# Seven products for eight in half of an input projection

## The reference

```python
xn = _rmsnorm(x, n1g)
z = xn @ w_in                       # 2048 x 6152: convolution B, C, x; q, k, v, o; two gates
bg, cg, xt, q, k, v, o, ig, fg = jnp.split(z, _SPLIT_IDX, axis=-1)
conv = causal_conv3(cg * xt);  y_conv = _rmsnorm(bg * conv, conv_g)
h, C1, n1, m1 = _mlstm_chunked(q, k, v, ig + b_i, log_sigmoid(fg + b_f), C0, n0, m0)
y_ml = sigmoid(o) * _rmsnorm(h, ml_g)            # per head, 4 heads
x = x + concat([y_conv, y_ml]) @ w_out
hn = _rmsnorm(x, n2g)
x = x + (silu(hn @ wg) * (hn @ wu)) @ wd         # feed-forward, 5632 wide
```

## Time and profile before

| | |
|---|---|
| median of 3 runs | 2466.73 us (2466.65 to 2467.93) |
| profiled execution, its own time | 2466.16 us |
| its span, first to last instruction | 2464.4 us |
| TensorE busy, matmuls | 2444.1 us (99%), 17544 |
| VectorE busy | 1760.1 us (71%) |
| ScalarE busy | 894.7 us (36%) |
| memory traffic | 132 GB/s over the span |

### The profile page before, as it was taken

The page is one execution under the profiler, slowest core; times in us unless marked ns, Lnnn a source line. Parts: engine busy times, 40 slices in busy tenths (PEclk is TensorE's granted clock), DMA queues, the critical chain, the costliest instruction groups (busy, mean ns, idle before and its releaser), DMA issues.

```text
span 2464.4 us, 44130 instructions
## 1 busy us (share of the span) xinstructions
PE 2444.1 (99%) x17544; PEld 2380.3 (97%) x17544; DVE 1760.1 (71%) x2453; ACT 894.7 (36%) x1235; POOL 48.3 (2%) x79
## 2 busy tenths in 40 slices
PE   9999999999999999999999999999999999999998
PEld 8999999999999998999999999999999999999886
DVE  7576585675687678778877877787777866866535
ACT  5222222122233335443344344434344533544313
POOL 0010000000000000000000000000000000000100
PEclk9999999999999999999999999999999999999999
DMA  5443343343336575443443434434334655745822
GB/s 132 118 132 89 114 120 95 85 134 95 105 101 184 174 210 174 120 120 111 128 119 104 128 111 121 118 112 121 117 101 116 246 153 160 264 129 144 286 73 77
DMA packets 459979, 329.09 MB, mean 134 GB/s; under 512 B 14407, under 2 KB 429283, under 8 KB 457425
## 3 DMA queue, kind: packets, MB, share of 16 engines
q1 hardware_dynamic: 403704, 250.29, 34.7%
q10 hardware_dynamic: 51448, 58.42, 7.6%
q0 software_dynamic: 4640, 17.73, 2.1%
HBM read 268.02 MB, written 58.37 MB: 132 GB/s over the span
## 4 chain that ended last, share of the span: by engine, by line
PE 60%; DVE 1%; ACT 0%; issue 0%; DVEq 0%; ACTq 0%
PE ps L838 17%; PE ps L842 17%; PE ps L840 17%; PE ps L853 2%; PE ps L956 2%; PE ps L958 2%; PE ps L960 2%; PE ps L983 0%; PE ps L964 0%; PE ps L965 0%; DVE oplo L2153 0%; PE ps L865 0%; DVE gw_ring L2140 0%; DVE dwlo L2409 0%; ACT ophi L1314 0%
## 5 line engine op out<-in xcount | busy, mean ns | idle before, releaser
L838 PE MATMUL ps<-ophi,gw_ring 128*128 128x288 f32 x3208 | 950.4, 296 | 5.0 <-DVE up L2197 3.5
L840 PE MATMUL ps<-oplo,gw_ring 128*128 128x288 f32 x3208 | 947.0, 295 | 0.0
L842 PE MATMUL ps<-ophi,gw_ring 128*128 128x288 f32 x3208 | 945.4, 295 | 0.0
L838 PEld LDWEIGHTS ps<-ophi,gw_ring 128*128 128x128 f32 x3208 | 602.4, 188 | 6.1 <-DVE up L2197 3.9
L842 PEld LDWEIGHTS ps<-ophi,gw_ring 128*128 128x128 f32 x3208 | 604.9, 189 | 0.0
L840 PEld LDWEIGHTS ps<-oplo,gw_ring 128*128 128x128 f32 x3208 | 603.1, 188 | 0.1
L1039 ACT ACTIVATE whi<-wraw 128x512 fp32r<-128x512 f32 x256 | 160.6, 632 | 576.2 <-PE ps L608 369.1
L605 PE MATMUL ps<-xhi,whi 128*128 128x288 f32 x1536 | 332.3, 298 | 0.5 <-DVE wlo L1612 0.5
L608 PE MATMUL ps<-xhi,wlo 128*128 128x288 f32 x1536 | 328.6, 296 | 0.0
L605 PE MATMUL ps<-xlo,whi 128*128 128x288 f32 x1536 | 328.5, 295 | 0.0
L2140 DVE TENSOR_TENSOR gw_ring<-graw_a,gw_ring 128x1024 fp32r<-128x1024 f32 x191 | 233.6, 1223 | 111.4 <-ACT gw_ring L1292 110.8
(11 more groups left out here) (339 smaller groups left out, 2669.9 us busy)
## 6 DMA issues: line engine op xcount, KB each, us to landing
wraw<-in_w_in_dram SPq DMA_DIRECT2D x96, 512.0 KB, 3.9
graw_a<-in_w_ffn_gate_dram SPq DMA_DIRECT2D x59, 512.0 KB, 3.7
graw_a<-in_w_ffn_up_dram SPq DMA_DIRECT2D x59, 512.0 KB, 4.7
graw_a<-in_w_ffn_down_dram SPq DMA_DIRECT2D x42, 512.0 KB, 5.8
wraw<-in_w_out_dram SPq DMA_DIRECT2D x32, 512.0 KB, 4.0
opraw<-hop SPq DMA_DIRECT2D x14, 1152.0 KB, 11.5
graw_b<-in_w_ffn_gate_dram SPq DMA_DIRECT2D x29, 512.0 KB, 3.8
graw_b<-in_w_ffn_up_dram SPq DMA_DIRECT2D x29, 512.0 KB, 4.7
```

The source lines that it names most:

```text
L838: pe.matmul(out, gw_ring[:, slot, 0, k, :], ophi[p][:, k, :], start=start and k == 0, stop=False, skip_group_check=True)
L840: pe.matmul(out, gw_ring[:, slot, 0, k, :], oplo[p][:, k, :], start=False, stop=False, skip_group_check=True)
L842: mm = pe.matmul(out, gw_ring[:, slot, 1, k, :], ophi[p][:, k, :], start=False, stop=k == GK - 1, skip_group_check=True)
```

## The change

The column tiles of a head are taken in six pairs: (q, k), (v0, v1), (o0, o1), (C, x) of group 0, (B of group 0, C of group 1), (x, B) of group 1. In 18 of the 24 pairs (`seven`) half of the K tiles, those of quarters 0 and 1, are multiplied as 2 x 2 blocks: rows are the two column tiles, the inner index is the quarter (0 or 1), columns are the two halves of the tokens. Seven products of blocks, each four K tiles by 288 columns, replace eight. Quarters 2 and 3 (d0, d1 of the first tile, d2, d3 of the second) are multiplied as before. The slots of a pair and the weight block of each:

The other six pairs keep eight quarters of 24 matmuls. A p slot has 12 matmuls, a d slot 24. TensorE's part:

```diff
+            def half_product(n, name, bank, start, stop, ready=None):
+                pe.wait_ge(lo_done, n + 1)
+                if ready:
+                    pe.wait_ge(*ready)
+                ...
+                for k in range(4):
+                    pe.matmul(out, whi[:, w, k, :], hi[:, k, :], ...)
+                    pe.matmul(out, whi[:, w, k, :], lo[:, k, :], ...)
+                    mm = pe.matmul(out, wlo[:, w, k, :], hi[:, k, :], ...)
+                mm.then_inc(w_used, 1)
+
+            def seven_pair(h, p, early=None, mid=None):
+                ...
+                before = (tile_read, i + 1) if not seven(*PLAN[PLAN.index((h, p)) - 1]) else (a_read, 2 * g)
+                pe.wait_ge(tile_read, i)
+                half_product(n, "p1", "c", True, False)
+                half_product(n + 1, "p0", "a", True, False, before)
+                direct_part(n + 2, 2, (("b", 0, True, False, None), ("c", 1, False, False, (copy_q, 3 * g + 1))))
+                if early:
+                    early()
+                half_product(n + 3, "p2", "a", False, False, (copy_q, 3 * g + 2))
+                half_product(n + 4, "p3", "b", False, False)
+                direct_part(n + 5, 3, (("b", 0, False, True, None), ("c", 1, False, False, None)))
+                if mid:
+                    mid()
+                half_product(n + 6, "p4", "a", False, False, (copy_q, 3 * g + 3))
+                half_product(n + 7, "p5", "c", False, True)
+                direct_part(n + 8, 2, (("d", 1, True, False, (tile_read, i + 1)), ("a", 0, False, False, (a_read, 2 * g + 1))))
+                half_product(n + 9, "p6", "a", False, False)
+                direct_part(n + 10, 3, (("a", 0, False, True, None), ("d", 1, False, True, None)))
```

The banks are a = 0, d = 1, b = 2, c = 3. ScalarE copies bank c after p1 and bank a after p0 and p2 (`copy_bank`, counted by `copy_q`), multiplies the norm gain into six of the eight weight quarters (`quad_gain`, four instructions of 128x128 each) and makes eleven high parts. VectorE makes the sums of weight blocks (`weight_total`), the gains of d0 and d1, eleven low parts, and builds the four result blocks:

```diff
+            def quad_gain(h, p, name):
+                ...
+                for k in range(4):
+                    ins = act.mul(raw_slot[j][:, k, :], raw_slot[j][:, k, :], vecs[:, col + k:col + k + 1])
+                ins.then_inc(quad_ok, 1)
...
+                def c11(h, p, out):
+                    slot_done(slot_of(h, p, "d1"))
+                    dve.wait_ge(copy_q, 3 * g + 2)
+                    link(tt(p1s[:], ps[:, 2, 0:HT], p1s[:], ALU.add))
+                    return out(p1s[:], 0)
+                def u3(h, p):
+                    slot_done(slot_of(h, p, "p4"))
+                    tt(p5s[:], ps[:, 0, 0:HT], p5s[:], ALU.add).then_inc(a_read, 1)
+                def c12(h, p, out):
+                    slot_done(slot_of(h, p, "p5"))
+                    link(tt(u2s[:], ps[:, 3, 0:HT], u2s[:], ALU.add))
+                    evac(out(u2s[:], 1))
+                def c21_c22(h, p, out):
+                    slot_done(slot_of(h, p, "d3"))
+                    out(ps[:, 0, 0:HT], 0).then_inc(a_read, 1)
+                    dve.wait_ge(a_read, 2 * g + 1)
+                    link(tt(p5s[:], ps[:, 1, 0:HT], p5s[:], ALU.add))
+                    evac(out(p5s[:], 1))
```

The order is written out by `step(h, p, s)`, which on VectorE does what slot s + 5 of the pair needs (a sum or a gain) and then the low part of slot s + 4; on ScalarE the bank copy, the high part of slot s + 4, and after some a `quad_gain` for a later slot. Pairs 3, 4 and 5 on VectorE, in a head with `seven(h, 3)` (steps without side work are joined):

```diff
+                    step(h, 3, 0)            # then conv_columns(0), states(), step 1, normaliser_parts(),
+                    ...                      # step 2, values_by_sample(), step 3
+                    steps(h, 3, 4, 5)
+                    first_half(h, 3, by_root(cg))
+                    steps(h, 3, 6, 7)
+                    c12(h, 3, by_root(cg))
+                    gate_again(6)
+                    step(h, 3, 8)
+                    denominator()
+                    step(h, 3, 9)
+                    c21_c22(h, 3, by_tile(cg, cg))
+                    step(h, 3, 10)
+                    outputs_of_head()
+                    step(h, 4, 0)
+                    conv_prompt(0, T)
+                    step(h, 4, 1)
+                    conv_sample(0)
+                    step(h, 4, 2)
+                    conv_scaled(0)
+                    step(h, 4, 3)
+                    sample_update()
+                    steps(h, 4, 4, 5)
+                    ...
+                    steps(h, 5, 2, 3, 4, 5)
+                    link(c11(h, 5, by_tile(cg, cg)))
+                    conv_prompt(0, HT)
+                    u3(h, 5)
+                    step(h, 5, 6)
+                    mixed_heads()
+                    step(h, 5, 7)
+                    c12(h, 5, by_tile(cg, cg))
+                    conv_prompt(HT, T)
+                    step(h, 5, 8)
+                    conv_sample(1)
+                    conv_scaled(1)
+                    step(h, 5, 9)
+                    c21_c22(h, 5, by_tile(own_conv(1), cv))
+                    step(h, 5, 10)
```

More of the change, by code:

```diff
@@ new lines, in hybrid_trunk_step @@
+    N_GAIN = len(GAINS)
+    QUADS = ("a21", "a22", "a11", "a12", "d2", "d3")
+    SUMS = ("p1", "p2", "p4", "p5")
+    NQ = 6
+    LOADS, free_at, loads_of = [], [0] * NQ, [0] * NQ
+    RAW_AT = {}
+    for h, p in PLAN:
+        if seven(h, p):
+            order = (("a21", "p4"), ("a22", "p6"), ("a11", "p4"), ("d0", "d0"), ("a12", "p5"), ("d1", "d1"),
+                     ("d2", "d2"), ("d3", "d3"))
+        else:
+            order = tuple((s, s) for s in QUARTERS)
+        for name, until in order:
+            j = min(range(NQ), key=lambda j: free_at[j])
+            loads_of[j] += 1
+            LOADS.append((h, p, name, j, free_at[j]))
+            RAW_AT[h, p, name] = j, 16 * loads_of[j]
+            free_at[j] = slot_of(h, p, until) + 1
@@ new lines, in gemm @@
+                for n in range(KT):
+                    w = ring(n0 + n // 4)
+                    if n % 4 == 0:
+                        pe.wait_ge(lo_done, n0 + n // 4 + 1)
+                    if n in between:
+                        between[n]()
+                    if ready:
+                        ready(n)
+                    k, (out, first, last) = ks[n], where[n]
+                    for moving in (hi, lo):
+                        for a in halves:
+                            pe.matmul(out[:, a, :], whi[:, w, n % 4, :], moving[:, 2 * k + a, :],
+                                      start=first and moving is hi, stop=False)
+                    for a in halves:
+                        mm = pe.matmul(out[:, a, :], wlo[:, w, n % 4, :], hi[:, 2 * k + a, :],
+                                       start=False, stop=last)
+                    if n % 4 == 3:
+                        mm.then_inc(w_used, 1)
@@ new lines, in direct_part @@
+            def direct_part(n, q, parts):
+                pe.wait_ge(lo_done, n + 1)
+                w = ring(n)
+                for bank, a, start, stop, ready in parts:
+                    if ready:
+                        pe.wait_ge(*ready)
+                    out = ps[:, BANK_T[bank], 0:HT]
+                    for s in range(4):
+                        k = 2 * (4 * q + s) + a
+                        pe.matmul(out, whi[:, w, s, :], xhi[:, k, :], start=start and s == 0, stop=False,
+                                  skip_group_check=True)
+                        pe.matmul(out, whi[:, w, s, :], xlo[:, k, :], start=False, stop=False, skip_group_check=True)
+                        mm = pe.matmul(out, wlo[:, w, s, :], xhi[:, k, :], start=False, stop=stop and s == 3,
+                                       skip_group_check=True)
+                mm.then_inc(w_used, 1)
@@ new lines, in steps, with hi_out @@
+            def steps(h, p, *which):
+                for s in which:
+                    step(h, p, s)
+            def hi_out(n, q):
+                if q < 2:
+                    act.wait_ge(raw_in[q // 2], n * 16 + 16)
+                else:
+                    act.wait_ge(gained, n * 2 + (N_GAIN + q - 1))
+                act.wait_ge(w_used, n * 4 + (N_IN + q + 1))
+                act.activation(whi[:, q], wraw[:, q // 2, 4 * (q % 2):4 * (q % 2) + 4, :], ACT.Copy).then_inc(hi_done, 1)
@@ L1213, in _ @@
+                mix_high(14)
+                squares_of_y(1)
+                mix_high(15)
+            for h in range(H):
+                round_of_head(h)
             act.wait_ge(rows_out, 1)
```

1234 lines of the change are left out of this document (767 added, 467 removed).

## The result

The changed kernel takes 2472.49 us (median of 18 runs, 2468.07 to 2475.02), the kernel before 2467.01 us in the same sessions (18 runs, 2466.06 to 2468.9): the ratio is 1.0021, 95% interval 1.0014 to 1.0028. It is slower by 5.5 us, just past the 0.2% named ahead. The forecast was 2463 us, range 2441 to 2476, with more chance on faster than on slower: the time lies in the range, on the side that had 0.24.

The account below looks back on a forecast made before the run. TensorE, busy 99% and issuing without holes, was taken as the bound: 2466.16 - 28.8 (matmuls) + 21.6 (waits) + 2.6 (clock) + 1 (late loads) = 2462.6; the runs' median stands 0.6 above that execution, so 2463 us, range 2441 to 2476.

Parts of the forecast that it names:

- the 0.2% named ahead: Threshold for no change: 4.9 us; faster meant below 2461.8 us, slower above 2471.7 us.
- the side that had 0.24: Chance given to slower than 2471.7 us: 0.2 from Rival (c) and 0.04 from rival (b); faster had 0.46.
- 28.8 us less for 216 matmuls: TensorE in 18 of 24 pairs: 12 matmuls fewer per changed pair, each saving 0.1333 us.
- An ordinary pair holds: Changed pairs without long side work: VectorE keeps up, with 1.9 us of slack before the next pair's sum.
- Rival (c): ScalarE becomes the bound in every changed pair, at the a22 quarter before the next pair's sum: 2478 us, chance 0.2.
- TensorE waits 4.5 us, in three heads: 13.5 us: End of pair 5: next pair's p0 waits for VectorE's C21 read, at 17.3 us where 12.8 is allowed.
- 1.4 + 0.2 + 0.8 + 0.3 = 2.7, three heads: 8.1 us: Pair 3 into 4: TensorE waits 1.4 at p0, 0.2 for `h_ok`, 0.8 at d2; u3 0.3 late.
- Late loads, "I take 1": Behind state store and spill, an 8 us landing pushes pair 4 by some 1.7 us; bounds 0 and 5, taken 1.
- The clock, "I take the middle, 2.6": Half clock after the three pair-5 waits, 1.7 us lost in one earlier event; bounds 0 and 5.1, taken 2.6 us.
- rival (b): All long waits drop the clock and loads come late: 2465 to 2468 us, no change, chance 0.23.
- signs named ahead: 17328 matmuls; pair-5 waits of 4.5 us then clock 0.5; 1.4 and 0.8 in pair 4; VectorE over 75%, ScalarE near 60%.
- three signs that were to show the forecast wrong: Pair-5 waits under 2 us; waits named after ScalarE's high parts or weight DMAs; spacing inside a product not 0.1333 us.

Follow-up runs that it names:

- one move out of pair 5: Changed kernel with the head's final products (`mixed_heads`) moved from pair 5 into the first step of the next head's pair 0: 2458.71 us, ratio 0.9966.
- work in the wait: Changed kernel with TensorE transposing a constant tile 30 times between p1 and p0 of pair 0, heads 1 to 3: 2467.32 us, ratio 1.0000.
- reordering only: Changed kernel with three VectorE moves: u3 of pair 5 earlier, state updates in two groups, first reciprocal behind pair 3's last evacuation: 2469.23 us, ratio 1.0007.
- state store later: Changed kernel with the sample-state store one pair later and a head's second spill behind the mixed outputs' signal: 2472.39 us, ratio 1.0017.
- C21 first: Changed kernel with pair 5's C21 scaled and read out of bank 0 before the second half's taps and sample taps: 2466.17 us, ratio 0.9995.
- buffer free early: C21 first, plus the sum for C22 written early into another buffer so `p5s` is freed: 2455.42 us, ratio 0.9955.
- and the transfers moved: Buffer free early, plus rows spread and spill behind pair 4's last low part and state store after step 7 of pair 5: 2447.32 us, ratio 0.9912.
- all that proved free: Kernel of "and the transfers moved" plus the three moves of "reordering only"; `mixed_heads` stays in pair 5: 2443.82 us, ratio 0.9903.
- everything in VectorE's list: Changed kernel with `mixed_heads` in next pair 0, C21 first, the "reordering only" moves, and sample-state products after p3; stores stay: 2460.76 us, ratio 0.9973.
- and the transfers: Everything in VectorE's list, plus rows spread and spill after pair 4's last low part, state store after step 7 of pair 5: 2452.51 us, ratio 0.9938.
- and the buffer free: Kernel of "and the transfers" plus early C22 sum in another buffer, head's outputs after p3's low part, sample-state products after d1: 2457.46 us, ratio 0.9963.
- more work for ScalarE: Changed kernel with each scaled copy on ScalarE done in two halves of 64 columns: 2481.22 us, ratio 1.0058.

## Why the forecast was wrong, by its own steps

- **28.8 us less for 216 matmuls** held. An undisturbed changed pair shows it: pair 1 of heads 1 to 3 takes 26.22 us instead of 27.96, pair 2 26.64 instead of 28.36, both 1.7 less, where twelve matmuls make 1.6.
- **"An ordinary pair holds"**, by 1.9 us, held: no wait in pairs 1 to 3, and 4.4 us more of ScalarE work lengthened them by 0.5 us at most. Rival (c) is out.
- **"TensorE waits 4.5 us, in three heads: 13.5 us"** held in size (12.65) and place. The reason was right as far as it went: work ahead of the read of C21. The forecast took all of it as having to stand there. It did not: with two releases (bank 0 and `p5s`) earlier in the same list the waits went, and no work had to leave. That `p5s` held a second wait behind the first was not seen.
- **"1.4 + 0.2 + 0.8 + 0.3 = 2.7, three heads: 8.1 us"** became 8.6: 1.24 at p0, 1.62 at d2, nothing at the other two.
- **Late loads, "I take 1"** is the step that failed most. I put the landing of 8 us behind the store and the spill on pair 4; it fell on pair 5, on d0, a quarter that VectorE must scale itself before the low part of p0 and the read of bank 0 can follow in its list. It cost 1.2, 0.6 and 1.7 us at p0 and then another 1.0 at u3, 6.4 us by the trace and 8.1 by the run with the transfers moved, for the 1 us of the sum. The upper bound was 5.
- **The clock, "I take the middle, 2.6"**: all three long waits were followed by half clock, 5.1 us by the records, 5.2 by the run that filled the waits. One event had shown the full price, and the middle stood on no row.
- Left over: 1.7 us outside the heads' stage, 0.6 ahead of it and 1.1 in the feed-forward stage. That stage, which no kernel here changes, takes 1537.5 to 1540.3 us in the fourteen profiles, so nothing shows that the change brought them.

So 25.2 us of waits, clock and load were forecast and 32.8 came, where 28.8 had been saved: a gain of 3.6 us became a loss of 4.0 in the stage. The late load brought 5.4 of the difference, the clock 2.5. The forecast named this case as rival (b), "all long waits drop the clock and loads come late", 2465 to 2468. Its own terms give more: 2463 - 3.6 + 5.1 + 3 to 5 is 2467.5 to 2469.5, so this range was added up some 2 us too low. What carried the time past even that was the late load, 1.4 us over its upper bound, and the 1.7 us outside the stage.

That the time lies in the stated range is no merit of the sum: the range is 35 us wide, and of the 0.24 on the side of slower, 0.20 stood on ScalarE as the bound, which it was not. Of the signs named ahead, the waits, their places and the matmul count came as written and VectorE had 75% of the heads' stage; ScalarE had 51% of it, not 60, since six of its pairs do not change. None of the three signs that were to show the forecast wrong came: no sign had been named for a late load that VectorE, not ScalarE, waits for.

The length of the heads' stage in the profiled executions, free of what happens outside it, puts the kernels nearly in the order of the medians. Only the reordering alone and the later store stand on the other side of the changed kernel, by 0.5 and 2.1 us, so neither is shown to help there (us):

| kernel | heads' stage | kernel | heads' stage |
|---|---|---|---|
| before | 687.5 | changed | 691.4 |
| one move out of pair 5 | 678.5 | work in the wait | 687.2 |
| reordering only | 691.9 | state store later | 693.5 |
| C21 first | 685.9 | buffer free early | 676.1 |
| and the transfers moved | 667.8 | all that proved free | 665.5 |
| everything in VectorE's list | 681.4 | and the transfers | 672.2 |
| and the buffer free | 678.0 | more work for ScalarE | 699.8 |

## What to carry to other kernels

When an engine gets more work in the shadow of another, list for each buffer and bank who frees it, and put these releases first in the busy engine's list: here the same work in another order was worth 17 us and moving a part of it behind them 14, and that move cost again once the order was right. A wait that is removed ahead of a fixed date (a landing, the end of a queue) comes back there, so remove the last one first. Put large stores where the loads are few: 3 MB in the burst of weight quarters cost 8 us, and a store moved by one pair into the next burst gained nothing.

## What the runs showed of the hardware

- The distance of two matmul starts has two values. In the output projection, without its few longer gaps, it was 0.1333 us in twelve of the fourteen profiles and 0.1300 in two (C21 first; everything with the free buffer), and the whole stage of 1549 matmuls took 202.7 us instead of 207.5. The heads' stage of the same two profiles kept 0.1333. The runs of the kernel with the free buffer fall into two groups some 5 us apart (2453.2 and 2453.6 beside 2457.5 to 2459.7), of which the profile is in the lower; those of C21 first spread without a gap over 2461.5 to 2470.4. That the groups are the two distances is likely and not shown, since only one execution of each was profiled. The same stretch, the changed kernel and then the one with C21 first; both at full clock:

```profile
760.00:780.00 20.00, 20.00 (x153) 20.00 (x152) 14.81 (x24) 6.04 (x11) 0.00 (x0) 1.00 0.65 201
```

```profile
760.00:780.00 20.00, 20.00 (x156) 20.00 (x156) 14.65 (x24) 7.07 (x12) 0.00 (x0) 1.00 0.76 227
```

  The Trainium skill (TensorE: Matmul & The Clock Gate, Back-to-back issue gap) gives columns / 2.4 + 2.5 ns for an isolated gap, 122.5 ns for 288 columns; neither value is that. What chooses between them is open.
- The same wait costs a different amount of clock. Behind the 3.5 us wait at the start of the feed-forward stage the clock was at half for 3.4 us in eight profiles, for 6.8 in five and not at all in one (the fastest kernel). Behind a wait of 2.1 us for the input in the prologue it fell in the changed kernel and did not in the one with the buffer free. In the heads' stage it fell behind every wait of 4.2 us and more, behind 3.0 us in one of three heads (C21 first), and behind 2.3 us in two of three (everything at once, the second kernel). The length of the wait alone does not decide: with more work for ScalarE it fell behind all three waits of 2.1 us and behind one of three of 3.5. The Trainium skill (TensorE: Matmul & The Clock Gate, What's actually happening) calls the low clock the default that activity releases; the runs agree, and the filled wait most plainly.
